# Expert products of a hybrid trunk: three split products of 128 tokens become plain fp32 products in four column tiles

## The reference, cut to what matters

```python
def moe(h, w_r, b_r, w_gu, w_down):
    logits = (t @ w_r).astype(jnp.float32) + b_r.astype(jnp.float32)
    top_v, top_i = lax.top_k(logits, TOP_K)
    wts = jax.nn.softmax(top_v, axis=-1)
    comb = jnp.sum(jax.nn.one_hot(top_i, N_EXPERTS) * wts[..., None], axis=1)
    for e in range(N_EXPERTS):
        out = out + comb[:, e:e + 1] * swiglu(t, w_gu[e], w_down[e])
```

## Time and profile before

| | us |
|---|---|
| median of 3 runs (1981.35 to 1981.62) | 1981.36 |
| the profiled execution's own time | 1976.57 |
| its span, first to last instruction | 1974.4 |

### The profile page before, as it was taken

The page is one execution under the profiler, slowest core; times in us unless marked ns, Lnnn a source line. Parts: engine busy times, 40 slices in busy tenths (PEclk is TensorE's granted clock), DMA queues, the critical chain, the costliest instruction groups (busy, mean ns, idle before and its releaser), DMA issues.

```text
span 1974.4 us, 33543 instructions
## 1 busy us (share of the span) xinstructions
PE 1923.0 (97%) x12982; PEld 1627.6 (82%) x12982; DVE 1565.5 (79%) x2210; ACT 1135.9 (58%) x1385; POOL 239.6 (12%) x279
## 2 busy tenths in 40 slices
PE   7999999999998999999999999999999999999997
PEld 3778998899997778988888888888888888888885
DVE  5896457655674976287999989989899898998995
ACT  2214344545432243344777877877778777777774
POOL 2550422000006332340000000000000000000000
PEclk9999999999999999999999999999999999999998
DMA  9576345555552664444799999999999999999993
GB/s 351 186 285 236 131 159 181 196 181 182 179 174 69 203 222 141 167 150 153 269 363 365 353 323 349 368 359 357 324 342 363 365 352 343 334 363 371 345 346 119
DMA packets 143063, 524.12 MB, mean 265 GB/s; under 512 B 16192, under 2 KB 16704, under 8 KB 142272
## 3 DMA queue, kind: packets, MB, share of 16 engines
q1 hardware_dynamic: 140544, 508.82, 71.3%
q10 hardware_dynamic: 1728, 7.90, 1.2%
q0 software_dynamic: 640, 5.35, 0.7%
HBM read 515.57 MB, written 6.43 MB: 264 GB/s over the span
## 4 chain that ended last, share of the span: by engine, by line
PE 85%; DVE 10%; ACT 3%; issue 2%; DMA 1%; ACTq 0%; DVEq 0%
PE bank L1044 28%; PE bank L1069 14%; PE bank L882 12%; PE bank L291 9%; PE bank L622 8%; PE bank L486 4%; DVE wlo L2417 3%; PE bank L502 2%; PE bank L969 2%; PE bank L1031 1%; ACT whi L1411 1%; DVE arena L1581 1%; PE bank L451 1%; PE bank L428 1%; DMA masks<-in_masks 1%
## 5 line engine op out<-in xcount | busy, mean ns | idle before, releaser
L2417 DVE TENSOR_TENSOR wlo<-ring,whi 128x1024 fp32r<-128x1024 f32 x756 | 910.4, 1222 | 144.8 <-ACT whi L1411 142.9
L1411 ACT ACTIVATE whi<-ring 128x1024 fp32r<-128x1024 f32 x756 | 799.9, 1060 | 293.2 <-PE bank L1044 145.3
L1044 PE MATMUL bank<-whi,gh 128*128 128x512 f32 x896 | 285.6, 400 | 2.2 <-DVE wlo L2417 0.9
L1044 PE MATMUL bank<-whi,gl 128*128 128x512 f32 x896 | 279.6, 393 | 0.0
L1044 PE MATMUL bank<-wlo,gh 128*128 128x512 f32 x896 | 278.8, 392 | 0.0
L291 PE MATMUL bank<-hT,ring 128*128 128x264 f32 x864 | 204.3, 396 | 5.0 <-issue 3.0
L1044 PEld LDWEIGHTS bank<-wlo,gh 128*128 128x128 f32 x896 | 168.2, 188 | 38.9
L291 PEld LDWEIGHTS bank<-hT,ring 128*128 128x128 f32 x864 | 165.9, 195 | 40.7 <-issue 11.9
L1044 PEld LDWEIGHTS bank<-whi,gl 128*128 128x128 f32 x896 | 168.1, 188 | 38.0
L1044 PEld LDWEIGHTS bank<-whi,gh 128*128 128x128 f32 x896 | 159.6, 188 | 32.3 <-DVE wlo L2417 3.2
L1069 PE MATMUL bank<-whi,eh 128*128 128x512 f32 x448 | 142.5, 399 | 0.3
(11 more groups left out here) (431 smaller groups left out, 3068.6 us busy)
## 6 DMA issues: line engine op xcount, KB each, us to landing
ring<-in_w SPq DMA_DIRECT2D x964, 512.0 KB, 5.2
out_gdns<-arena POOLq DMA_DIRECT2D x2, 2048.0 KB, 8.4
arena<-in_gdn ACTq DMA_DIRECT2D x2, 1536.0 KB, 7.2
xT<-in_x ACTq DMA_DIRECT2D x1, 1056.0 KB, 8.9
out_y<-hT SPq DMA_DIRECT2D x4, 264.0 KB, 2.1
arena<-in_gdn ACTq DMA_DIRECT2D x2, 512.0 KB, 3.8
masks<-in_masks ACTq DMA_DIRECT2D x1, 512.0 KB, 11.0
cpk<-in_cpk SPq DMA_DIRECT2D x1, 512.0 KB, 6.4
```

Of the source, the lines that this page charges most:

```text
L1044: ins = pe.matmul(o[half], x[:, k, mine], w[part][:, CH * half:CH * half + CH], start=k == 0 and n == 0, stop=k == KD - 1 and n == 2)
L1411: act.activation(whi[:, m % SPL, :], ring[:, r, :], ACT.Copy).then_inc(sem("hi_done"), 1)
L2417: v.tensor_tensor(wlo[:, m % SPL, :], ring[:, (low.base + m) % RING, :], whi[:, m % SPL, :].bitcast(F32), ALU.subtract).then_inc(sem("lo_d ...
```

## The change

Every expert product is made in plain fp32 from the slot as it landed, so ACT's `whi`, DVE's `wlo`, `gl` and `el` go. `CAP` becomes 96: three held tiles (`TT`) of 32 tokens. The array is used as four column tiles of 32. Each slot is streamed once for a held tile, as four quarters of 256 columns, each quarter in another column tile: 3 x 4 = 12 matmuls of 32 held and 256 moving columns. `whi` and `wlo` were 8 places of a slot; their space becomes `ring2`, so the experts' ring has `ERING` = 14 slots. SP may load a slot again when PE has used it (`e_used`). The result of a down product lies in three banks and is first copied to `ys` (three copies by ACT, three by DVE) before it is scaled. The places of the small pieces move, and combine does two tiles after each of four slots. Gathers use 192 columns instead of 256, in two banks instead of six at the start.

```diff
-CAP = 128
+CAP = 96
-NCH = FF // CH
+NCH = FT // 4
+ERING = 14
+TT = CAP // 32
+DQ = D // 4
...
+        ring2 = over("ring2", [P, ERING - RING, SLOT * P], where(whi), 0, F32)
...
-        TURN = 6
         LAG = SPL - 1
-        ROWS = 2
-        COMBINE = range(3, 11)
-        DCT = 11
+        TURN = 3
+        ROWS = 0
+        COMBINE = range(4, 8)
+        DCT = 9
...
+        def up_bank(c, r):
+            return bank[TT * (c % 2) + r]
+
+        def down_bank(r):
+            return bank[TT + r]
+
+        def quarter(j, r):
+
+            return (j, r) if j < TT else (r, TT)
...
+                def slot_products(s, x, first, last):
+
+                    w = place(s)
+                    for r in range(TT):
+                        for j in range(4):
+                            t, c = quarter(j, r)
+                            o = up_bank(s // KD, r) if s < UP_S else down_bank(r)
+                            ins = pe.matmul(o[32 * j:32 * j + 32, 0:DQ], x(t), w[:, DQ * c:DQ * c + DQ],
+                                            start=first, stop=last)
+                    ins.then_inc(sem("e_used"), 1)
...
                 for s in range(UP_S):
                     c, k = s // KD, s % KD
-                    pe.wait_ge(sem("lo_done"), q * FFN_S + (base + s + 1))
-                    if k == 0 and c >= 2:
+                    pe.wait_ge(place_sem(s), place_count(q, s))
...
-                    for n, (x, part) in enumerate(((gh, 0), (gh, 1), (gl, 0))):
-                        for half in range(2):
-                            ins = pe.matmul(o[half], x[:, k, mine], w[part][:, CH * half:CH * half + CH],
-                                            start=k == 0 and n == 0, stop=k == KD - 1 and n == 2)
...
             def expert_weights(q, e, s0, s1):
                 for s in range(s0, s1):
-                    sp.wait_ge(sem("lo_done"), q * FFN_S + (FFN_S + s - RING + 1))
-                    r = (MIX1_END + s) % RING
-                    sp.dma_start(ring[:, r, :], w_in[e * FFN_S + (MIX1_END + s)]).then_inc(landed[r], 16)
+                    if not (s0 and s < ERING):
+                        sp.wait_ge(sem("e_used"), q * FFN_S + (s - ERING + 1))
+                    sp.dma_start(place(s), w_in[e * FFN_S + (MIX1_END + s)]).then_inc(place_sem(s), 16)
...
             for k in range(KD):
                 act.wait_ge(sem("x_mix"), KD + k + 1)
                 act.activation(xsq[:, k, :], xT[:, k, :], ACT.Square).then_inc(sem("sq_done"), 1)
-                if k >= KD - LAG:
-                    s = k - (KD - LAG)
-                    n = MIX1_END + s
-                    high(n % RING, 16 * (n // RING + 1), s, FFN_S + s + 1)
...
+            p(pool.memset(yh[:, :].bitcast(F32), 0.0))
+            p(pool.memset(yl[:, :].bitcast(F32), 0.0))
```

More of the change, by code:

```diff
@@ L268, in trunk_program @@
         landed = [sem(f"landed{r}") for r in range(RING)]
+        landed2 = [sem(f"landed2_{r}") for r in range(ERING - RING)]
         used = sem("slots_used")
@@ L351, in trunk_program, with chunk_after, place, place_sem @@
         ADAS = [(0, 0)] + ADA_IN[0] + [ADA_LATE[0]] + ADA_IN[1] + [ADA_LATE[1]]
-        def silu_after(m):
-            return [c for c in range(NCH) if m == KD * (c + 1) + SPL - 1]
+        def chunk_after(m):
+            return [c for c in range(NCH) if m == KD * (c + 1)]
         def turned_after(m):
-            return [c for c in range(NCH) if m == KD * (c + 1) + TURN + SPL]
+            return [c for c in range(NCH) if m == KD * (c + 1) + TURN + 1]
+        def place(m):
+            p = m % ERING
+            return ring[:, (MIX1_END + p) % RING, :] if p < RING else ring2[:, p - RING, :]
+        def place_sem(m):
+            p = m % ERING
+            return landed[(MIX1_END + p) % RING] if p < RING else landed2[p - RING]
+        def place_count(q, m):
+            p = m % ERING
+            before = len([n for n in range(MIX1_END) if n % RING == (MIX1_END + p) % RING]) if p < RING else 0
+            return q * (16 * FFN_S // ERING) + 16 * (before + m // ERING + 1)
         Y_AFTER = [7, 11, 15]
@@ L955, in _, with gather @@
             class Experts:
-                def gather(self, i, pg, sets=2):
+                def gather(self, i, pg):
                     if i == 0:
                         pe.wait_ge(sem("dsel_done"), pg * 1 + 1)
-                    if i >= sets:
-                        pe.wait_ge(sem("gh_done"), pg * 4 + (i - sets + 1))
-                        pe.wait_ge(sem("gl_done"), pg * 4 + (i - sets + 1))
+                    if i >= 2:
+                        pe.wait_ge(sem("gx_done"), pg * 4 + (i - 1))
                     for m in (2 * i, 2 * i + 1):
[L967 to L970, removed]
+                        for t in range(3):
+                            for src in (hth, htl):
+                                ins = pe.matmul(bank[6 + i % 2][:, PAIR * (m % 2):PAIR * (m % 2) + PAIR],
+                                                src[:, t, m * P:(m + 1) * P], dsel[:, t, :], start=t == 0 and src is hth,
+                                                stop=t == 2 and src is htl)
                     ins.then_inc(sem("gather_full"), 1)
@@ L1023, in turn @@
                 def turn(c):
                     pe.wait_ge(sem("act_done"), q * NCH + (FT + 1 + c + 1))
[L1026 to L1032, removed]
+                    if c:
+                        pe.wait_ge(sem("turned_done"), q * NCH + c)
@@ L1057, in expert @@
                         for t in range(3):
                             m = P if t < 2 else NB
-                            ins = pe.transpose(bank[4][0:CAP, P * t:P * t + m], dw[0:m, t, :], ident[0:m, 0:m])
+                            ins = pe.transpose(bank[7][0:CAP, P * t:P * t + m], dw[0:m, t, :], ident[0:m, 0:m])
                         ins.then_inc(sem("dcT_full"), 1)
[L1061 to L1075, removed]
@@ new lines, in expert @@
+                for f in range(FT):
+                    s, c, i = UP_S + f, f // 4, f % 4
+                    pe.wait_ge(place_sem(s), place_count(q, s))
+                    if f == 0:
+                        pe.wait_ge(sem("dcT_done"), q * 1 + 1)
+                    if i == 0:
+                        pe.wait_ge(sem("turned_done"), q * NCH + (c + 1))
+                    at = lambda t: P * i + 32 * t if i < TT else P * t + CAP
+                    slot_products(s, lambda t: ea[:, c, at(t):at(t) + 32], f == 0, f == FT - 1)
+                    if f == TURN:
@@ L2295, in choose, with rows, low @@
                     ins.then_inc(sem("dsel_done"), 1)
-                def gathered(self, i, pg, sets=2):
-                    v.wait_ge(sem("gather_full"), pg * 4 + (i + 1))
-                    v.tensor_copy(gl[:, 2 * i:2 * i + 2, :], both(bank[2 * (i % sets) + 1])).then_inc(sem("gl_done"), 1)
-                def rows(self, g):
+                def rows(self, g, q, a):
+                    v.wait_ge(sem("ywt_done"), g + 1)
+                    if a is not None or q:
+                        v.wait_ge(sem("e_used"), q * FFN_S)
+                    for r in range(TT):
+                        ins = v.tensor_copy(ys[32 * r:32 * r + 32, TT * DQ:D], down_bank(r)[CAP:P, 0:DQ])
+                    ins.then_inc(sem("e_ys"), 1)
+                def low(self, g):
                     for half in range(2):
@@ L2320, in begin @@
                     self.choose(0, a)
-                    for i in range(4):
-                        self.gathered(i, pg, 3 if a is None else 2)
-                    v.memset(ywt[:, :], 0.0).then_inc(sem("ywt_done"), 1)
-                    for half in range(2):
-                        v.memset(bank[6 + half][0:CAP, :], 0.0).then_inc(sem("ye_full"), 1)
+                    v.memset(ywt[:, :], 0.0)
+                    for r in range(TT):
+                        ins = v.memset(down_bank(r)[:, 0:DQ], 0.0)
+                    ins.then_inc(sem("ywt_done"), 1)
                     if a is None:
@@ L2376, in __call__ @@
                     expert(self, q, g, pg, e, sub, a)
-            four = lambda b: b[:, 0:4 * CAP].rearrange("p (a b) -> p a b", b=CAP)
             def expert(self, q, g, pg, e, sub, a):
                 for m in range(FFN_S):
-                    if not (a is None and e == 0 and m < LAG):
-                        low(m, q * FFN_S + (FFN_S + m + 1))
-                    for c in silu_after(m):
+                    if m == ROWS:
+                        self.rows(g, q, a)
+                        self.low(g)
@@ L2393, in expert @@
[L2393 to L2400 removed]
+                        for r in range(TT):
+                            ins = v.tensor_tensor(erow[:, c % 2, r, :], srow[:, c % 2, r, :], up_bank(c, r)[:, P:2 * P], ALU.mult)
```

195 lines of the change are left out of this document (96 added, 99 removed).

## The result

The changed kernel takes 1936.29 us (median of 4 runs, 1935.6 to 1937.91) against 1981.49 (1981.35 to 1981.7): ratio 0.9773, 95% interval 0.9756 to 0.979, 45 us faster. The prediction said 2007, slower, with a range of 1935 to 2045 and 0.63 on slower. Its direction was wrong; of its cases the first rival (PE stays the bound, 1943) is the one that came. The range holds 1936, by 1.3 us, because it had been stretched down to 1935 for that rival; the forecast's own range, 1977 to 2042, does not.

The account below looks back on a forecast made before the run. PE was taken to bound the kernel, DMA after the change. One engine's 849 + 128 x 1.45, with 2 for end products, made 1037 for 1007.7: +29, -1 around it, taken as +26: 1981.4 + 26 = 2007, range 1935 to 2045.

Parts of the forecast that it names:

- the first rival: Expert stage: packets spread over engines or hidden under the deep ring, PE sets 971 us, kernel 1943; chance 0.20.
- the forecast's own range: Whole kernel: one engine, 1.3 to 1.6 us a packet, base 1.27 to 1.31 a slot: 1977 to 2042; chance 0.62.
- What bounded the kernel before: Expert stage before the change: PE sets the pace, 1.50 us a slot over 1007.7 us, DMA close behind.
- PE's parts: Expert products: six packs of four column tiles, 1.31 us a slot, 880 us for 672; with pieces and switches 971.
- Small pieces and switches: PE in the expert stage: turns, combinations, gathers and short waits stay 62 us; interrupting column tiles adds 29.
- The 0.26 for an interruption: PE leaving and entering the column tiles: 0.13 us each, 14 times an expert, 3.6 us, 29 in all.
- ACT and DVE: Their removed split passes hid under PE, worth almost nothing; small gains and losses around the stage net -1 us.
- DMA's base and the count of packets: Expert stage: 658 slots landing at 1.29 us take 849 us; instruction packets rise from 37 to 128.
- The cost of a packet: One 16 KB instruction packet delays its DMA engine by 0.96 to 1.6 us, taken as 1.45.
- so I take one engine with 3 to 1: Expert stage: all PE instruction packets go to one DMA engine, 849 + 128 x 1.45 = 1035 us, making DMA the bound.
- the prediction's own two alternatives: Where packets go: round all 16 engines, DMA needing 861 us, or always to one engine, needing 1035 us.
- "spread" case: Expert stage: packets go round 16 engines, each losing 12 us; DMA needs 861 us and PE stays the bound.

Follow-up runs that it names:

- the merged kernels: Changed kernel with small pieces put together, 10 interruptions an expert instead of 14: 1923.21 us; with turns of two chunks also together, 8 interruptions: 1918.09 us.
- one_tile: Changed kernel with only the first of three rounds of products, 4 matmuls a slot instead of 12, every slot still loaded: 1826.22 us.
- narrow: Changed kernel with all 12 matmuls a slot, each with 128 moving columns instead of 256: 1838.25 us.
- by_count: Changed kernel with pieces and double turns put together, PE reading token counts and making two held tiles for experts of at most 64 tokens: 1897.01 us.

## Why the prediction was wrong

**What bounded the kernel before** was right: PE, and with DMA close behind.

**PE's parts** were right, within about 1%. Column tiles run side by side with 256 columns; the 1.31 us a slot was 1.295, the lower part of its range (870 us for 672 slots instead of 880). Small pieces and switches together were 962.2 - 870.2 = 92 us, where 62 + 29 = 91 stood. The 0.26 for an interruption was small: by the merged kernels it is 0.31, or 35 us for 112, and the pieces themselves then 57 instead of 62. The figure of the Trainium skill (TensorE: Matmul & The Clock Gate, Part 3), three column tiles at 2.38 times one, would have given 1.63 a slot at the same efficiency; for four tiles in a long stream the trace doesn't agree. Fourteen plain fp32 records of the mixer with the whole array held stand in PE's timeline of the changed kernel so (L297, the L291 of before; one lasts 0.39):

```profile
143.13 3.28 PE L297 MATMUL bank<-hT,ring 128*128 128x264 f32 x14
```

That is (3.28 - 0.39)/13 = 0.222 us a record, 0.84 ns a column; a pack of four column tiles, 0.2158 us for 256 columns, has 0.84 too. Four tiles cost what one full record costs, without loss.

**ACT and DVE** were right: in the stage no row of PE's waits names either.

**DMA's base and the count of packets** were right: 128 against 131, and one_tile's stage came at 853.7 where 849 for slots and 4 for spread packets were put.

**The cost of a packet** was right too, 1.45 us on its engine against 1.5 in the single cases.

**The step that failed** is one sentence: "so I take one engine with 3 to 1". What stood for it was that packets of one queue follow one another and never overlap. That says that one is fetched at a time, not on which engine, and nothing in it spoke against sixteen. In its place the runs show eight engines taking the packets by turns. The term 128 x 1.45 = 186 us was eight times too large; on each of eight engines it is 23 us, and 849 + 23 = 872 is under PE's 962, and close to narrow's 869.2, where that sum can be read. Of the prediction's own two alternatives the truth lies between, but both its "spread" case and the true one leave PE as the bound, so the first rival's time stands: 971 - 1 made 1943, and 1936 was measured, with a stage of 962.

What would have told the two cases apart is whether two packets delay the same share or different ones. The expert stage of before could hardly show it: while slots stream, its packets start 18.7 to 33.9 us apart, and the lag of the one at 1233.8 (one share from 1.23 to 2.63 us behind the first) is gone after some 10 us. It needs a stage with many packets or with DMA as the bound. So the odds of 3 to 1 had no measurement behind them.

The Trainium skill (Runtime: NRT & Kernel Launch, Instruction fetch mechanics) calls the crossing of an instruction block mostly hidden. In the changed kernel the trace agrees: 131 packets, no wait of PE. In narrow, where DMA is the bound, it doesn't: 0.18 us a packet.

Not settled: why eight engines and which. Whether the number is eight in other programs no run here shows.

## What to carry to other kernels

When a change multiplies a small cost, the factor to check first is not the cost but where it falls: a resource that is used by turns divides it. A rival's number can be taken to the chip cheaply by making the suspected engine the bound (leave work out elsewhere) and varying only the count of the suspected events. With column tiles, work that leaves them should be brought together, since each interruption costs about as much as three transposes (0.27 to 0.31 us for 0.32); and tokens should be held in steps of 32, as few as the data needs.

## What the runs showed of the hardware

Instruction packets of 16 KB delay eight of the sixteen shares of a slot strictly by turns (all 47 packets of one_tile's stage), which is read as eight of the sixteen DMA engines taking them in rotation, and each delays its engine's share of the weights by about 1.5 us, though it is under way for only about 1.0 us by the queue's share in the earlier trace rows. The changed kernel loads one every 7.3 us (962 us, 131 packets) with no harm to PE.

A jump over a long piece of PE's program costs it 4.9 to 6.1 us, two in a row 9.9 (by_count).

Four column tiles of 32 held columns in plain fp32 take 0.84 ns a moving column together, what one record with the whole array held takes.

When PE has only a third of its products (one_tile), the granted clock in the stage falls to 0.78, and the time is still set by DMA:

```profile
950.00:1790.00 840.00, 618.55 (x5780) 190.01 (x5776) 100.29 (x338) 85.55 (x275) 0.00 (x0) 0.78 1.02 408
```
